# Two edits to a two-layer encoder trunk: the first weight transfers wait for x and for each other, and the two heads of a pair are transposed back to back

## What is computed

```python
for i in range(DEPTH):                       # DEPTH = 2
    mix = even_mixer(...) if i % 2 == 0 else odd_mixer(...)
    h = layer_norm(ALPHA * h + mix, ...)
    h = layer_norm(ALPHA * h + memory_attention(h, mem, ...), ...)
    ffn = swiglu(...) if i % 2 == 0 else moe_swiglu(...)      # 8 experts, top 2
    h = layer_norm(ALPHA * h + ffn, ...)

# even_mixer: 8 heads of sliding-window attention with sinks (softmax over exp),
#             8 heads of stick-breaking attention (products of sigmoids)
# odd_mixer:  16 heads of forgetting attention (softmax with a cumulated gate)
# memory_attention: k, v = split(mem @ wkv); softmax(q k^T) v @ wo
```

## Time and profile before

| | |
|---|---|
| median of 3 runs | 1654.12 us (1653.77 to 1656.69) |
| the profiled execution, its own time | 1656.39 us |
| its span, first to last instruction | 1654.6 us |
| PE busy | 1607.6 us, 97% |
| DVE busy | 1271.3 us, 77% |
| ACT busy | 1035.9 us, 63% |
| mean granted clock of TensorE | 0.990 |
| read from memory | 473.54 MB |

### The profile page before, as it was taken

One profiled execution on the slowest core, in us unless ns is written; L12 is line 12 of the kernel. 1 busy time (PEld: TensorE's weight loads), 2 busy tenths in 40 slices (PEclk: granted clock), 3 DMA queues, 4 the chain that ended last, 5 costly groups with the idle time before them and its releaser, 6 DMA issues.

```text
span 1654.6 us, 21339 instructions
## 1 busy us (share of the span) xinstructions
PE 1607.6 (97%) x7602; PEld 1323.1 (80%) x7602; DVE 1271.3 (77%) x1180; ACT 1035.9 (63%) x935; POOL 108.3 (7%) x121
## 2 busy tenths in 40 slices
PE   8999989999999999899999999999999999999997
PEld 7777878888787788688888888888888888888775
DVE  5687564555646675789889889889888988988996
ACT  4464544443436544677777777777777777777673
POOL 2002010000112201000000000000000000000120
PEclk9999999999999999999999999999999999999999
DMA  9536645455455462899999999999999999999992
GB/s 332 178 102 217 241 152 183 149 215 192 157 190 190 151 203 82 278 386 356 389 377 377 389 369 372 388 369 387 389 360 380 388 370 386 388 356 390 362 371 93
DMA packets 238104, 480.11 MB, mean 290 GB/s; under 512 B 8224, under 2 KB 11328, under 8 KB 238048
## 3 DMA queue, kind: packets, MB, share of 16 engines
q1 hardware_dynamic: 229744, 454.06, 76.4%
q0 software_dynamic: 6288, 21.63, 4.1%
q10 hardware_dynamic: 2016, 3.67, 0.6%
HBM read 473.54 MB, written 11.03 MB: 293 GB/s over the span
## 4 chain that ended last, share of the span: by engine, by line
PE 89%; DVE 7%; issue 2%; ACT 1%; DMA 1%; DVEq 0%; SPq 0%; ACTq 0%
PE bank L378 27%; PE bank L380 27%; PE bank L379 27%; PE bank L844 1%; PE bank L422 1%; DVE w_lo L1937 1%; PE bank L665 1%; PE bank L643 1%; DVE X L1482 1%; DVE w_lo L1445 1%; DVE X L1491 1%; PE bank L538 1%; DMA raw<-in_ab_w_in_dram 1%; PE bank L558 0%; DVE stats L1471 0%
## 5 line engine op out<-in xcount | busy, mean ns | idle before, releaser
L1077 ACT ACTIVATE w_hi<-raw 128x2048 fp32r<-128x2048 f32 (+1 forms) x322 | 608.6, 1895 | 234.5 <-PE bank L380 224.4
L1937 DVE TENSOR_TENSOR w_lo<-raw,w_hi 128x2048 fp32r<-128x2048 f32 x221 | 503.1, 2290 | 81.9 <-ACT w_hi L1077 78.6
L1445 DVE TENSOR_TENSOR w_lo<-raw,w_hi 128x2048 fp32r<-128x2048 f32 (+1 forms) x96 | 210.9, 2202 | 138.0 <-ACT w_hi L1077 137.9
L378 PE MATMUL bank<-w_hi,xe_hi 128*128 128x512 f32 x736 | 293.0, 398 | 1.1 <-DVE w_lo L1937 1.1
L380 PE MATMUL bank<-w_hi,xe_lo 128*128 128x512 f32 x736 | 288.0, 391 | 0.0
L379 PE MATMUL bank<-w_lo,xe_hi 128*128 128x512 f32 x736 | 287.3, 390 | 0.0
L378 PE MATMUL bank<-w_hi,xT_hi 128*128 128x512 f32 (+1 forms) x560 | 219.1, 391 | 4.9 <-DVE w_lo L1445 4.3
L379 PE MATMUL bank<-w_lo,xT_hi 128*128 128x512 f32 (+1 forms) x560 | 214.6, 383 | 0.0
L380 PE MATMUL bank<-w_hi,xT_lo 128*128 128x512 f32 (+1 forms) x560 | 214.6, 383 | 0.0
L380 PEld LDWEIGHTS bank<-w_hi,xe_lo 128*128 128x128 f32 x736 | 138.5, 188 | 30.0
L378 PEld LDWEIGHTS bank<-w_hi,xe_hi 128*128 128x128 f32 x736 | 138.6, 188 | 28.6 <-DVE w_lo L1937 1.5
(11 more groups left out here) (282 smaller groups left out, 2143.2 us busy)
## 6 DMA issues: line engine op xcount, KB each, us to landing
raw<-in_moe_w_gate_dram SPq DMA_DIRECT2D x96, 1024.0 KB, 9.0
raw<-in_moe_w_up_dram SPq DMA_DIRECT2D x96, 1024.0 KB, 8.4
raw<-in_moe_w_down_dram SPq DMA_DIRECT2D x96, 1024.0 KB, 6.8
raw<-in_mem_wkv_dram SPq DMA_DIRECT2D x16, 1024.0 KB, 5.0
raw_more<-in_moe_w_up_dram SPq DMA_DIRECT2D x16, 1024.0 KB, 8.6
raw_more<-in_moe_w_gate_dram SPq DMA_DIRECT2D x16, 1024.0 KB, 8.7
raw_more<-in_moe_w_down_dram SPq DMA_DIRECT2D x16, 1024.0 KB, 7.4
raw<-in_c_w_in_dram SPq DMA_DIRECT2D x12, 1024.0 KB, 5.1
```

The source lines that it names most:

```text
L378: nc.tensor.matmul(d, xh, hi[:, k, :], start=(first and k == 0), stop=False)
L1077: return nc.scalar.activation(dst, src, ACT.Copy)
L1445: tt(w_lo[s][:, 0:n], raw[c % NRAW][:, 0:n], w_hi[s][:, 0:n].bitcast(F32), ALU.subtract).then_inc(lo_made, 1)
L1937: tt(w_lo[s][:, :], raw_exp[r][:, :], w_hi[s][:, :].bitcast(F32), ALU.subtract).then_inc(lo_made, 1)
```

## The change

Part one (SP): before chunk 2 is issued, SP waits until both halves of x have landed; before chunk 3 until chunk 0 has landed; before chunk 4 until chunk 1 has landed. The memory tokens are issued one chunk later, after chunk 3. Part two (PE, both layers): `second(2p - 2)` and `second(2p - 1)` come one right behind the other, ahead of the kv rows of both steps, where before each came behind the kv rows of its step.

```diff
@@ attention, both layers, PE
                     if p >= 2:
                         values(p - 2)
                     for i in (2 * p, 2 * p + 1):
+                        if p >= 1:
+                            second(i - 2)
+                    for i in (2 * p, 2 * p + 1):
                         mem_kT(i)
                         mem_kv(i)
-                        if i >= 2:
-                            second(i - 2)
@@ weight chunks, SP
             for c, (src, n, cols) in enumerate(chunks):
-                if c == NSPL:
+                if c == 2:
+
+                    for half in range(2):
+                        sp.wait_ge(sem(f"x_in{half}"), 16)
+                elif 2 < c <= 4:
+                    sp.wait_ge(raw_in[c - 3], 16)
+                if c == NSPL + 1:
                     sp.dma_start(mem_tok[:, :, :], mem[0].rearrange("(t p) d -> p t d", p=P))\
                       .then_inc(sem("mem_in"), 16)
```

## The result

The changed kernel took 1662.51 us in the median of 7 runs (1659.43 to 1664.36); the kernel before, in 7 runs beside it, 1655.67 (1653.77 to 1661.31). The ratio is 1.0038, 95% interval 1.0025 to 1.005: slower by 0.25 to 0.5%, some 6 us. The forecast was 1656.8, with 1653.0 to 1660.5 as the range. The sign of the sum was right, its size was not. The profiled execution took 1661.12 us (span 1659.4), against 1656.39 (1654.6).

The account below looks back on a forecast made before the run. PE, busy 97% of the span, was taken as the bound, its waits paid nearly whole. The terms -1.1 + 0.8 + 3.0 = +2.7 us on the median 1654.12 gave 1656.8 us, 8-in-10 range 1653.0 to 1660.5.

Parts of the forecast that it names:

- Term 1: Start: PE goes on past the memory tokens at 19.4 instead of 20.46 us, -1.1 us, bounds +0.5 and -2.1.
- the gain: Start: chunk 0 lands at 9.2 instead of 10.63 us, so PE reaches the memory tokens 1.4 us earlier, at 19.1.
- The loss: Start: the memory tokens, now fifth megabyte in the queue, land at 19.3 us, between 18.4 and 20.9.
- rival A: Start: the hold brings nothing, PE waits for tokens landing at 20.9; +0.5 instead of -1.1 us, total 1658.4; chance 0.17.
- Term 2: Layer 0's attention: PE 2.9 us behind at pair 4, 2.1 given back at the end; +0.8 us, bounds -1.0 and +2.5.
- Term 3: Layer 1's attention: newly uncovered waits of PE delay the out product; +3.0 us, bounds +1.0 and +5.5.
- rival B: Layer 1: the clock falls, two pairs' kv rows run at half rate; 2 x 1.4 us more, total 1659.6; chance 0.12.
- Rival C: Attention: early transposes remove the late waits at both layers' ends, -2.3 us each, total 1648.4; chance 0.11.

Follow-up runs that it names:

- warm_old: The kernel before with 14 idle matmuls instead of 8 behind the transposes of x; median 1655.08 us, ratio 0.9995.
- warm_hold: The kernel before with 14 idle matmuls instead of 8 behind the transposes of x, plus SP's whole edit; median 1656.98 us, ratio 1.0012.
- filled: The changed kernel with idle matmuls ahead of the waiting transposes in layer 0's pair 1 and layer 1's pairs 1 and 2; 1657.94 us, one run.
- pe_l0_late: The kernel before with PE's new order only from pair 4 of layer 0 on; median 1654.88 us, ratio 0.9988.
- pe_only: The kernel before with PE's new order in both layers' attention, SP's order as before; median 1659.91 us, ratio 1.0023.
- pe_layer0: The kernel before with PE's new order in layer 0's attention alone, SP's order as before; median 1655.57 us, ratio 0.9995.
- pe_layer1: The kernel before with PE's new order in layer 1's attention alone, SP's order as before; median 1663.58 us, ratio 1.0052.

## Why the prediction was wrong

**What bounds the kernel** was right: PE's work stayed what it was (1608.2 us), and a wait of PE's at the three places went through to the end.

**Term 1, the start, had the wrong sign.** I wrote that with chunks 0 and 1 alone under way chunk 0 lands at 9.2 and the sum is -1.1. The failed step is the gain: it took the 10.63 of one trace as the time that the old order gives, and explained it by the transfers behind it. Eight traces of the old order gave 8.7 to 10.6. I had also missed that the clock stood at 0.50 behind chunk 0 in that trace (13 to 16.5 us), up to 1.7 us of its 28.11 that other executions don't have. The loss was sized about right: the tokens landed at 18.9 to 20.1 (I took 19.3). That choice within its bounds was luck: no run shows that the engines run less far ahead of each other with a shorter queue, and the lower bound was summed too low (five megabytes are 5.24 MB, which leaves 3.0 and not 2.9 behind 10 us, so 18.7). Without a gain to set against, that delay is the result: chunk 3 is 1.3 us later in the mean of all traces, and `warm_old` against `warm_hold` shows it in the medians as well, 1655.08 and 1656.98. That was rival A, +0.5 there. The ring order that the Trainium skill states ("DMA: Bandwidth & Descriptors", Queues, rings and completion order) agrees with these traces: chunk 0, which stands ahead of all that was held back, gained nothing that shows when less was queued behind it.

**Term 2, layer 0, was +0.8 and measured -0.5.** The wait of 4 us and the low clock behind it came as worked out: at the scores of pair 4 PE was 2.8 us behind (I had 2.9), of which `filled` gives 1.1 to the clock (I had 1.5). The end gave back 2.3 (I had 2.1). Off was pairs 4 to 7: I let nothing be gained there, and they caught up 1.0 us; `pe_l0_late` shows these pairs and the end to be worth 1.6 alone. The -0.5 is that of two traces (after, `pe_only`); `pe_layer0`, with a fall twice as long, has +0.9, so the +0.8 lies inside what one order gives.

**Term 3, layer 1, +3.0, measured +5.9, above its upper bound of 5.5: this step failed the prediction.** It priced the kv rows behind the new waits at full clock; they ran at 0.50 in pair 2, and its small waits were too small. The order of waits, pair by pair, was right. The scores of pairs 2 to 7 came late by this much, relative to the first scores:

| pair | 2 | 3 | 4 | 5 | 6 | 7 | out product |
|---|---|---|---|---|---|---|---|
| predicted | +2.0 | +2.7 | +2.5 | +3.4 | +3.2 | +3.6 | +3.0 |
| after | +2.2 | +4.7 | +4.6 | +5.6 | +5.5 | +6.1 | +5.9 |
| after, clock kept up (`filled`) | +2.2 | +3.1 | +3.0 | +4.0 | +3.9 | +4.5 | +4.4 |

The columns part at one place, the kv rows of pair 2, by 2.0 us; 1.6 of it is the clock, and nearly all of that is carried to the end (1.5). I had named that fall and set it aside as rival B, with 0.12, because the row at 524 us of the kernel before showed a similar wait (1.43 us) without one. The same trace has a nearer case that I overlooked: behind the 2.28 us before 558.43, as long as the waits that I forecast, the clock did fall. Before, columns as above:

```profile
559.00:560.00 1.00, 1.00 (x10) 0.81 (x7) 1.00 (x1) 0.58 (x3) 0.00 (x0) 0.58 0.00 0
560.00:561.00 1.00, 1.00 (x6) 0.87 (x5) 0.93 (x5) 0.00 (x0) 0.00 (x0) 0.50 0.00 0
```

That fall has its counterpart in after from 563 us on (1.7 us lost in both), so it is no part of the 5.9. The other 1.4 of the 2.9 are small pieces: 0.2 at pair 1, another 0.1 or 0.2 at each pair after it, 0.9 together, and an end that gave back 0.1 and not 0.6. The wait for ACT's copy stayed (2.03 us at 561.78 against 2.28), with ACT's `w_hi` of step 13 still ahead of it, and 1.05 us of waiting for DVE at the last transposes came on top. What makes up the small pieces was not tested one by one. The gate that the Trainium skill describes ("TensorE: Matmul & The Clock Gate", Part 1) was the right rule to weigh more: the kv rows at 529 to 532 us stood at 0.50 behind a wait of 1.93 us, though those behind the 2.10 us of pair 1 did not.

**The sum** was +2.7. With the terms as measured it is +1.3 (the mean of the starts, not the one pair of traces), -0.5 and +5.9, so +6.7, beside 6.3 from the ratio. Rival C's gain at the end of layer 0 was there; what it left out was layer 1's `w_lo`, as written against it.

## What to carry to other kernels

Work that does not depend on a wait is its cover. Moving an instruction ahead of that work cost time here where the engine that it waits for had something long of its own queued first, a `w_lo` of 2.29 us, and gained in layer 0's later pairs; so try such a turn pair by pair, not for a whole loop. A single trace of a start says little about transfers: look at several executions of the same order before a landing time is given a cause. And a newly exposed wait should be priced both with the clock kept up and with it fallen, without taking one similar wait that was spared for a reason against the fall.

## What the runs showed that I had not expected

The clock does not fall in the same way each time, even for the same instructions. At the start, PE idle for 2.78 (after), 2.97, 3.03 and 3.86 us ahead of chunk 0 was followed by a clock of 0.50 (1.2 GHz); the ten other traces idled less than that, and in nine of them, `pe_layer0` with 2.39 us among them, the clock stayed at 1.00 (2.4 GHz). In the tenth, `pe_l0_late`, it fell behind 2.29 us; its timeline, and one of its stretches:

```profile
11.31 0.59 PE L378 MATMUL bank<-w_hi,xT_hi 128*128 128x512 f32 x1 [2.29 <-DVE w_lo L1449]
```

```profile
12.00:13.00 1.00, 1.00 (x4) 0.71 (x4) 1.00 (x2) 0.00 (x0) 0.00 (x0) 0.50 1.08 408
```

The 2.02 us in `warm_hold` were followed by a fall, the 2.10 us at 519.97 of after were not, the 1.93 at 527.65 again were. Such a fall at the start cost 1.7 us of full-clock work in every trace that had it (the length of the stretches times one less their clock); those in the attention cost 1.7 each too, or twice that (3.4 us in layer 0 of `pe_layer0` and at the end of layer 1 in `pe_layer1`, `pe_l0_late`, `warm_old` and `warm_hold`). What such a loss costs the kernel depends on who waits: 1.1 us in layer 0 and 1.5 in layer 1 with the new order (`filled`), nothing in layer 0 with the old one (`warm_hold`).

The landing of the first half-megabyte chunk wandered by 1.9 us between executions, with the same order on SP and the same bytes ahead of it.
